# No filler matmuls behind three norms of a two-layer decoder trunk

## What is computed

```
def _rmsnorm(x, g):
    y = xf * lax.rsqrt(jnp.mean(xf * xf, axis=-1, keepdims=True) + NORM_EPS)
    return (y * g.astype(F32)).astype(x.dtype)

def _hybrid_layer(h, ...):
    hn = _rmsnorm(h, g_mix_pre) * valid[None, :, None]
    u = hn @ w_in
    ... four token mixers, gated sum `merged` ...
    mix_out = merged @ w_out
    h = h + _rmsnorm(mix_out, g_mix_post)
    f = _rmsnorm(h, g_ffn_pre)
    ffn_out = (jax.nn.silu(f @ ffn_w_gate) * (f @ ffn_w_up)) @ ffn_w_down
    return h + _rmsnorm(ffn_out, g_ffn_post)
```

## Time and profile before

| | |
|---|---|
| time, median of 3 runs (lowest to highest) | 954.03 us (953.54 to 955.42) |
| time of the profiled execution | 953.93 us |
| its span, first to last instruction | 951.8 us |
| TensorE busy | 935.1 us (98%) |
| VectorE, ScalarE, GpSimd busy | 609.9, 507.4, 75.7 us |
| mean granted TensorE clock | 0.999 |

### The profile page before, as it was taken

How to read it: one execution, slowest core, us unless ns; L and a number is a source line. 1 busy time by engine, 2 the same in 40 slices (tenths; PEclk the granted TensorE clock), 3 DMA queues, 4 the chain that set the end, 5 groups by cost and what they waited for, 6 DMA issues and landing times.

```text
span 951.8 us, 18756 instructions
## 1 busy us (share of the span) xinstructions
PE 935.1 (98%) x7336; PEld 888.5 (93%) x7336; DVE 609.9 (64%) x926; ACT 507.4 (53%) x812; POOL 75.7 (8%) x67
## 2 busy tenths in 40 slices
PE   8999999999999999999999999999999899999998
PEld 7999988899989999999989998888999899999886
DVE  5866575367968655553478775754678776565543
ACT  5645654475457444444446447555854665554442
POOL 0000000000031222210100000000000312222000
PEclk9999999999999999999999999999999999999999
DMA  8585445356552655555545653444564636556652
GB/s 248 169 253 163 148 158 172 115 146 165 173 183 91 216 176 175 170 174 166 175 134 174 204 160 115 140 150 133 149 186 154 221 105 205 176 179 214 203 183 83
DMA packets 161004, 159.52 MB, mean 168 GB/s; under 512 B 3464, under 2 KB 153488, under 8 KB 160944
## 3 DMA queue, kind: packets, MB, share of 16 engines
q1 hardware_dynamic: 159344, 155.16, 52.4%
q10 hardware_dynamic: 1552, 3.39, 1.1%
q0 software_dynamic: 48, 0.13, 0.0%
HBM read 156.48 MB, written 1.06 MB: 166 GB/s over the span
## 4 chain that ended last, share of the span: by engine, by line
PE 89%; issue 3%; DMA 3%; DVE 3%; ACT 1%; POOL 0%; SPq 0%; DVEq 0%; POOLq 0%; ACTq 0%
PE banks L697 24%; PE banks L699 24%; PE banks L698 23%; PE banks L1083 2%; PE banks L1084 2%; PE banks L1082 2%; PE banks L730 1%; PE banks L738 1%; PE banks L731 1%; DVE lo L1545 1%; PE banks L948 1%; DMA raw<-in_w_in 1%; DMA raw<-in_ffn_w_gate 1%; ACT hi L1149 1%; DMA raw<-in_w_out 1%
## 5 line engine op out<-in xcount | busy, mean ns | idle before, releaser
L1545 DVE TENSOR_TENSOR lo<-raw,hi 128x1024 fp32r<-128x1024 f32 (+1 forms) x287 | 348.9, 1220 | 133.4 <-ACT hi L1149 132.3
L697 PE MATMUL banks<-xh,hi 128*128 128x272 f32 (+1 forms) x1440 | 416.0, 289 | 0.5 <-DVE lo L1545 0.3
L699 PE MATMUL banks<-xh,lo 128*128 128x272 f32 (+1 forms) x1440 | 411.7, 286 | 0.0
L698 PE MATMUL banks<-xl,hi 128*128 128x272 f32 (+1 forms) x1440 | 410.6, 285 | 0.0
L1149 ACT ACTIVATE hi<-raw 128x1024 fp32r<-128x1024 f32 (+1 forms) x281 | 293.5, 1048 | 130.3 <-PE banks L699 48.0
L697 PEld LDWEIGHTS banks<-xh,hi 128*128 128x128 f32 x1440 | 271.4, 188 | 6.9 <-issue 4.9
L699 PEld LDWEIGHTS banks<-xh,lo 128*128 128x128 f32 x1440 | 271.5, 189 | 0.0
L698 PEld LDWEIGHTS banks<-xl,hi 128*128 128x128 f32 x1440 | 271.0, 188 | 0.0
L1236 ACT ACTIVATE gates<-banks,par 128x272 f32<-128x272 f32 (+1 forms) x64 | 30.7, 480 | 94.1 <-PE banks L699 88.4
L2053 POOL TENSOR_TENSOR silu_g<-silu_g,rstd 128x272 f32<-128x272 f32 (+1 forms) x44 | 52.6, 1197 | 211.7 <-ACT silu_g L1425 211.7
L2046 POOL TENSOR_TENSOR sq<-sq 128x272 f32<-128x272 f32 (+1 forms) x18 | 22.2, 1232 | 593.3 <-ACT sq L1399 592.5
(11 more groups left out here) (254 smaller groups left out, 1393.1 us busy)
## 6 DMA issues: line engine op xcount, KB each, us to landing
raw<-in_w_in SPq DMA_DIRECT2D x54, 1024.0 KB, 5.3
raw<-in_ffn_w_gate SPq DMA_DIRECT2D x22, 1024.0 KB, 5.4
raw<-in_ffn_w_up SPq DMA_DIRECT2D x22, 1024.0 KB, 5.4
raw<-in_ffn_w_down SPq DMA_DIRECT2D x19, 1024.0 KB, 5.0
raw<-in_w_out SPq DMA_DIRECT2D x8, 1024.0 KB, 5.0
raw<-in_w_in SPq DMA_DIRECT2D x12, 512.0 KB, 4.3
raw<-in_w_branch SPq DMA_DIRECT2D x12, 512.0 KB, 5.5
raw<-in_ffn_w_down SPq DMA_DIRECT2D x4, 768.0 KB, 4.2
```

The costliest lines, as they stand in the source:

```text
L697: mm(dst, wh, mh, start=start, stop=False)
L698: mm(dst, wh, ml, start=False, stop=False)
L699: return mm(dst, wl, mh, start=False, stop=stop)
L1545: tt(half_of(lo, g, c), half_of(raw, g, c), half_of(hi, g, c).bitcast(F32), ALU.subtract).then_inc(lo_ready, 2 if g in G_MIX else 1)
```

## The change

The two calls of `keep_warm` inside the loop over layers go, so that 4 matmuls fewer run at A, B and C. The 8 at the start stay. `wait_taken` at B, which waited for bank 7 to be free, stays.

```
-WARM_START, WARM_NORM = 8, 4
+WARM_START = 8
...
                 mean_square(l, 1, q_start(l))
-                keep_warm(WARM_NORM)
                 gate_up(l)
...
                 mean_square(l, 3, q_start(l))
                 wait_taken(pe, TILE[l]["gu"] + 2)
-                keep_warm(WARM_NORM)
```

## The result

The changed kernel takes 958.66 us (median of 7 runs, 955.13 to 959.18), the kernel before 954.64 us (7 runs, 953.54 to 955.42). The ratio is 1.0033, 95% interval 1.0024 to 1.0043: slower, as forecast, by 3.15 us at the ratio's middle against 3.3 forecast; the two medians lie 4.02 us apart. The profiled execution took 957.25 us with a span of 955.3 us, 3.46 us more than the span before.

A forecast was written before the change was run, and what follows sets the result against it. TensorE, busy 935.1 of 951.8 us, was taken to bound the kernel. Direct gain 0, A +1.75, B 0, C +1.55 sum to +3.3 us on 953.93, giving 957.2 us, range 953.8 to 959.2.

The forecast's parts named there:

- A: Pause of TensorE behind the mean square ending at 282.54 us; 2.90 us without fillers, a fall priced at +1.75 us.
- B: Pause of TensorE behind the mean square ending at 487.72 us; 2.63 us without fillers, no fall expected.
- C: Pause of TensorE behind the mean square ending at 754.58 us; 3.22 us without fillers, a fall priced at +1.55 us.
- No direct gain: At A, B and C the removed fillers' 5.5 us of busy time lie beside the chain, so removing them gains 0.
- the rival that the fillers hold up the chain: At the three pauses, fillers slow ScalarE, VectorE or the next matmul; faster, deciding from 952.0 us; chance 0.03.
- The price of a fall: Behind a bared pause, dense work at 1.2 GHz until the clock rises loses 1.75 us, as at the start.
- the upper bound: Price of a fall at most 3.5 us, twice 1.75, if the clock rises one such stretch later.
- B at 0: No fall behind B, since its twin, the start's pause of 2.61 us, brought none; adds 0.
- two falls: The clock falls behind A and C only; 957.2 us, the likeliest case, chance 0.27.
- all three: Rival: the clock falls behind A, B and C, with little work ahead of each pause; 958.4 us, chance 0.20.
- Nothing given back elsewhere: Starts behind A and C shift by 1.4 to 1.75 us each; other engines' waits and transfers stand as they were.
- one place: Rival: a fall behind C only, or one on average over executions; 955.5 us, +0.16%; chance 0.25.

The follow-up runs named there:

- the last kernel: 11 fillers at the start instead of 8, 5 behind each mean square, 1 ahead at A, 2 at C; against the kernel before: 953.41 us, ratio 0.9989.

## Why the prediction was right, and where it was not

**No direct gain.** Right. The pauses kept the lengths that the chain through ScalarE and VectorE gives them: 2.63 and 3.22 us at B and C, to the hundredth as worked out. A's was 2.70 instead of 2.90. There VectorE's weight rest had begun earlier (282.41 instead of 282.69), and that belongs to the 0.28 us by which A came sooner. By my own sign, a pause shorter by more than 0.1, this would speak for the rival that the fillers hold up the chain. It doesn't: the kernel with four fillers at A and none at the start had 2.63 us there (284.74 to 287.37).

**The cause, the clock.** Right, and shown: the clock falls at the bared places and not behind those that keep their fillers, in each of the three kernels with one place bare. The fillers with 16 columns exclude that their mere presence does it.

**The price of a fall, 1.75 us.** Right in size behind A and C: +1.51 and +1.45, where 1.75 and 1.55 stood in the sum. The case of the upper bound, two stretches, also happened: behind A alone they cost 2.84 us, where the bound had 3.5.

**B at 0.** This step of the sum failed, and with it the likeliest case, two falls: what happened was the rival "all three", which stood at 958.4 us with a chance of 0.20. The median of 958.66 lies next to that and not to 957.2. The sum took B as the twin of the start's pause (2.63 against 2.61 us), which had brought no fall. B fell in every profile in which it was bare, and cost +1.80 us here, more than either of the others. The argument failed because one execution of one pause says little about its length. The same pause at the start, 2.06 us long, brought a fall in another execution. That B alone left the median where it was is no success of this step, since its reason was that the clock would not fall. That B's price is cushioned was right: one stretch cost +0.41 us alone. Two stretches cost +1.65 to +1.80 us, where dense work would have lost half of the 6.04 us under it, 3.02.

**Nothing given back elsewhere.** Failed too, and in the other direction. TensorE's wait ahead of C's mean square was 1.02 us shorter. I had taken it as fixed. It was 1.77 us with C alone bare, 0.80 with B alone, 0.57 in the changed kernel's second profile, 1.98 in the first with small fillers, and 0.75 with one filler, whose profile had no fall at all, so it does not follow the falls. ScalarE's timeline ahead of it, before (first) and after, names what it hangs on:
```profile
747.66 1.06 ACT L1149 ACTIVATE hi<-raw 128x1024 fp32r<-128x1024 f32 x1 [2.78 <-DMA raw<-in_ffn_w_gate]
```
```profile
749.65 1.06 ACT L1147 ACTIVATE hi<-raw 128x1024 fp32r<-128x1024 f32 x1 [1.79 <-DMA raw<-in_ffn_w_gate]
```
ScalarE waits for a weight group, the squares are queued behind that, and GpSimd adds them in series. The group was there 1.99 us later than before, but the last product ended 3.03 us later. I read this from the timelines; no run changed it alone. With the 0.28 us ahead of A it took back 1.30 of the 4.76 us. The forecast of +3.3 against +3.46 in the profile is therefore good partly by luck: two errors cancel, +1.80 and -1.30, and the execution was one of the quicker ones.

**What in the profile would show it.** The clock below 1.00 behind A and C came, and that behind B staying at 1.00 did not. The low clock behind B held for 6.83 us, nearly twice the 3.7 us of the start, which stood there as a sign of being wrong; A and C kept to 3.41. A start every 0.25 us was near: 0.21 to 0.23. The busy time "5.5 us lower, less what a low clock adds" came out as 0.1 us lower.

**The rule of the Trainium skill** that I had as the rival "one place" (the page "TensorE: Matmul & The Clock Gate", section "Why this matters for your kernels") would have let only C fall. The runs disagree: A fell at 2.70 us and B at 2.63.

**What stays open.** The start has a fall in some executions and not in others, and so have the places with one filler. No run separates what decides it; the low stretches began at other distances from the pause in nearly every profile. Open are also what moves the wait ahead of C, and what of the last kernel's gain is not the clock.

## What to carry to other kernels

Where the matrix engine waits some microseconds between two dense stages, filler work that ended before the wait did was free here, and 5.5 us of it in three places saved about 3 us. Its worth is a matter of chances per execution, so judge it by the mean clocks of many executions and the granted clock in windows of a few microseconds, and never infer from one pause in one trace that pauses of its length are harmless. Look for the same pauses elsewhere, the start and the wait ahead of the norm included: filling those as well gained 0.9 us more and left a spread of 0.7 us, though not all of that is shown to be the clock's.

## What the runs showed of the hardware that was not expected

- The fall can come after the work has resumed: 0.83 us after it at A, with six records at full rate between, and 1.35 us at A in the second profile with small fillers.
- All low stretches inside the program lasted 3.41 us or 6.83 us, twice that.
- The length of a pause does not decide alone. At the start 2.06 and 3.14 us brought a fall, while 2.61 us in the kernel before and 2.73 in the one with A alone bare brought none.
- A stretch at 1.2 GHz behind B cost 0.41 us for 3.00 us of work, since the tiles arrive there more slowly than TensorE takes them at full clock (in the kernel before ScalarE starts one every 1.24 to 1.25 us from 494.23 on; TensorE needs 1.12 to 1.13 for one); behind A the dense work lost nearly half of the stretch (2.84 of 6.18 us).
